# The looped last pair of experts in the order of the straight chunks

## The chip, the cores and the metric

The kernel runs on one core of a Trainium2 chip. The metric is device time in microseconds (us), from the first to the last instruction of one execution. Three executions of the kernel before took 1598.59, 1598.82 and 1604.25 us; their median is 1598.82 us.

## The reference, cut to what matters

The router picks 2 of 16 experts for each token. Two decoder layers with the same shape run one after the other over 576 tokens (512 of a prompt, 64 of a sample group). Each layer is a block of token mixers followed by a mixture of experts, with a layer norm after either. The change touches only the mixture of experts:

```python
def moe_ffn(h, w_router, b_router, w_gate, w_up, w_down):
    ...
    hg = jnp.einsum('ntd,edf->ntef', h, w_gate)
    hu = jnp.einsum('ntd,edf->ntef', h, w_up)
    act = jax.nn.silu(hg) * hu * combine[..., None].astype(h.dtype)
    return jnp.einsum('ntef,efd->ntd', act, w_down)
x = layer_norm(DN_ALPHA * x + f, lw['ln2_g'], lw['ln2_b'])   # f = moe_ffn(x, ...)
```

The width is 1024, an expert's hidden width 256, and all of it is float32.

## The kernel before

Tokens are sorted by expert into chunks of up to 128 rows, each chunk with one expert. Chunks 0 to 15 always exist, one per expert; an expert with more rows gets more chunks behind these. How many there are is only known when the router has run, so the first 14 chunks (`STATIC`) are written out straight, and the rest run in a hardware loop over pairs of chunks, whose trip count each engine reads from the tile `plan` (`pairs`, L1639). With these inputs the trip count is 1 in each layer: the page counts 32 gate-and-up loads in two layers. So a layer has chunks 0 to 15, and chunks 14 and 15 are the loop's only pair.

What a chunk n needs, and which engine does it (functions of `experts`, L1572):

- SP loads the gate and up weights (`load_gu`, 2 MB) and the down weights (`load_dw`, 1 MB), each into one of three slots.
- POOL gathers the chunk's rows from HBM by an indirect DMA (`gather`) and at the end adds the result rows into the output in HBM by another one (`scatter`). Scatters must not overlap, since two may add to one row: each waits until the one before has landed (`y_stored`).
- PE transposes the rows (`rows_t`, called for the chunk behind by `next_rows_t`), does the gate-and-up product (`gate_up`, 24 matmuls), transposes the hidden rows (`hidden_t`) and does the down product (`down`, 8 matmuls) into one pair of PSUM banks.
- ACT makes the high parts of the weights (`gate_up_high`, 4 casts: each float32 operand is split into a high and a low part) and of the rows (`rows_high`), the tanh of the gate (`gate_tanh`), the copy of the transposed hidden rows (`hidden_copy`) and the copy of the result out of PSUM (`output_copy`, which waits for the landing of the scatter two chunks back, since it overwrites its source).
- DVE makes the low parts of the weights and rows (`gate_up_low`, `rows_low`) and finishes the hidden rows (`hidden`).

The program writes every engine's order out by hand; semaphores do the rest. In the straight chunks the order is staggered. PE does `gate_up(n)`, `hidden_t(n-1)`, `next_rows_t(n)`, `down(n-1)`, and ACT and DVE split the weights of chunk n+1 while PE works on chunk n. In the loop it is not: chunk 13 is finished ahead of the loop, then the weights of 14 and 15 are split one after the other, and each of the two chunks goes through `gate_up`, `next_rows_t`, `hidden_t`, `down` before the next starts.

On POOL, which the change leaves as it is, the straight chunks gather four chunks ahead while there are straight chunks to gather for, and the loop, for a = 0 and 1, gathers chunk 16 + a and then scatters chunk 14 + a (L1856 to 1873):

```python
for n in range(STATIC):
    if n + 4 < STATIC + 2:
        pool.wait_ge(xt_done, n + 3)
        gather(n % 2, table[:, 0, n + 4:n + 5])
    pool.wait_ge(y_out, n + 1)
    ...
    scatter(n % 2, table[:, 1, n:n + 1])
with pool.Fori(0, pairs(pool)) as p:
    for a in range(2):
        ...
```

So straight chunks 12 and 13 gather nothing, and the gather for chunk 16 stands behind the scatter of chunk 13. Chunk 16 has no rows here, but PE transposes its (stale) row buffer all the same: `next_rows_t` of chunk 15 waits on `rows_in_a` for that gather.

When the last scatter has landed, SP reloads the summed rows (L2076), and the layer norm behind them begins.

Of the kernel before, what the change touches and what calls it, by code (L numbers as in the profile page):

```python
# [14 lines left out]
F32 = mybir.dt.float32  # L15
# [44 lines left out]
MAXCH = 24  # L60
# [5 lines left out]
for _n, _w in [("ident", 128), ("diag", 128), ("cos", NTT * 8), ("sin", NTT * 8), ("cm", NT * 32), ("cneg", NT * 32),  # L66
               ("newneg", 2 * 64), ("scneg", 2 * 128), ("bcur0", 4 * 128), ("bcur", 4 * 128), ("bprev", 4 * 128),
               ("bst", 4 * 64), ("bnew", 4 * 64), ("tri", 128), ("ones", 128), ("pairm", 32), ("th", 5),
               ("chunk", 32), ("gm", 128), ("gms", 64), ("blk", 4), ("rowhead", 4), ("mhalf", NTT), ("gsel", 256), ("lane", 128), ("row1", 1), ("tile128", 2 * NTT),
               ("pad", 2 * (MAXCH + 2)), ("e128", 16), ("over", 16), ("fix", 32)]:  # L70
    _C[_n] = (_at, _at + _w)
    _at += _w
# [12 lines left out]
def constants():  # L85
# [60 lines left out]
    put("tile128", np.tile(128 * (np.arange(2 * NTT) % NTT), (128, 1)))  # L146
    put("over", np.tile(128 * (15 - np.arange(16)), (128, 1)))
# [1408 lines left out]
class Chunk:  # L1556


    def __init__(self, n, slot, side, half, nth):
        self.n, self.slot, self.side, self.half, self.nth = n, slot, side, half, nth  # L1560


def fixed_chunk(c):
    return Chunk(c, c % RING_E, c % 2, c // 2, c // RING_E + 1)


def looped_chunk(p, a):
    c = STATIC + a
    return Chunk(p * 2 + c, c % RING_E, a, p + c // 2, p + (c // RING_E + 1))


def experts(k):  # L1572
# [18 lines left out]
    with ExitStack() as outer:  # L1591
# [4 lines left out]
        plan = so("plan", [1, 34], I32)  # L1596
        with ExitStack() as ctx:
# [14 lines left out]
            big, pf = sb("cmpbuf", [1, 32, E]), sb("plan_f", [1, 34])  # L1612
# [32 lines left out]
            def _(sp):  # L1645
                def load_gu(ch, e):
                    sp.dma_start(gu[:, ch.slot, :], io["we"][l, e, :, 0:4096]).then_inc(gu_in[ch.slot], 16)

                def load_dw(ch, e):
                    sp.dma_start(dw[:, ch.slot, :], io["we"][l, e, :, 4096:6144]).then_inc(dw_in[ch.slot], 16)  # L1650
                load_dw(fixed_chunk(2), 2)
                norm.load(sp)
                for n in range(RING_E, STATIC + 1):
                    if n < STATIC:
                        sp.wait_ge(gu_done, n - RING_E + 1)
                        load_gu(fixed_chunk(n), n)
# [15 lines left out]
            def _(pe):  # L1672
# [58 lines left out]
                def down(ch, first=False):  # L1731
# [4 lines left out]
                    pe.wait_ge(dw_in[ch.slot], ch.nth * 16)  # L1736
                    for n in range(2):
                        for f in range(2):
                            last = pe.matmul(ps[:, YB + n, :], hT[:, f, :],  # L1739
                                             dw[:, ch.slot, f * D + n * 512:f * D + (n + 1) * 512],  # L1740
# [12 lines left out]
                hidden_t(fixed_chunk(STATIC - 1))  # L1753
                down(fixed_chunk(STATIC - 1))
                with pe.Fori(0, pairs(pe)) as p:
                    for a in range(2):
                        ch = looped_chunk(p, a)
                        gate_up(ch)
                        next_rows_t(ch)
                        hidden_t(ch)  # L1760
                        down(ch)

            @block.scalar
            def _(act):
# [5 lines left out]
                def gate_up_high(ch, early=False, begin=0):  # L1770
                    act.wait_ge(gu_in[ch.slot], ch.nth * 16)
# [3 lines left out]
                    for q in range(begin, PIECES):  # L1775
                        cols = slice(q * PW, (q + 1) * PW)
                        act.copy(guH[ch.side][:, cols], gu[:, ch.slot, cols]).then_inc(w_hi, 1)  # L1777
# [98 lines left out]
            def _(dve):  # L1876
# [41 lines left out]
                def gate_up_low(ch, pieces=(0, 1, 2, 3)):  # L1918
                    for q in pieces:
                        cols = slice(q * PW, (q + 1) * PW)  # L1920
                        dve.wait_ge(w_hi, ch.n * PIECES + (q + 1))
                        dve.tensor_tensor(guL[:, ch.slot, cols], gu[:, ch.slot, cols], guH[ch.side][:, cols].bitcast(F32),  # L1922
# [58 lines left out]
                def plan_chunks():  # L1981
# [12 lines left out]
                    step(dve.memset(pf[:, 33:34], 0.0))  # L1994
# [194 lines left out]
```

## Time and profile before

| | us |
|---|---|
| median of three executions | 1598.82 |
| the profiled execution's own time | 1600.21 |
| span of its trace | 1598.5 |
| PE busy in the span (matmul) | 1411.0 |
| DVE busy | 780.1 |
| ACT busy | 607.6 |
| POOL busy | 178.1 |

The span is the stretch from the first to the last instruction in the trace. The experts of layer 1 lie between 565 and 775 us, those of layer 2 between 1363 and 1569 us. Below, "scatter 12" is the twelfth counted from 0, that of chunk 12, and so for all steps; POOL issues the scatters of even chunks from `y_a` and those of odd ones from `y_b`. A row of a timeline gives the start, the duration, the engine, the line, the operation with its tiles, how many were merged, and in brackets how long the engine had been idle and what ended that. For a DMA the duration is that of its issue; when its data have landed stands in the answers on DMA, in us from the issue.

### The profile page before, as it was taken

The numbers are of one execution on the slowest core, as the hardware profiler recorded it, in microseconds if no ns is written. First come the engines' busy times: TensorE is split into PE (matmuls) and PEld (weight loads), VectorE is DVE, ScalarE is ACT, GpSimd is POOL, SyncE is SP. The second block draws the span as 40 slices with busy tenths as digits, with TensorE's granted clock in tenths as the row PEclk, the third lists the DMA queues.
The fourth block names the chain that finished last, engine by engine and source line by source line (L and its number), as shares of the span: only waits on it lengthen the run. The fifth ranks groups of instructions, "written<-read, shape, count | busy, mean of one in ns | idle before, by whom it ended". The sixth has DMA issues, their size and how long they took to land. (4 is left out here: it accounts for less than half of the span.)

```text
span 1598.5 us, 22710 instructions
## 1 busy us (share of the span) xinstructions
PE 1411.0 (88%) x9068; PEld 1156.1 (72%) x9068; DVE 780.1 (49%) x1294; ACT 607.6 (38%) x1142; POOL 178.1 (11%) x154
## 2 busy tenths in 40 slices
PE   7999897999999779987289998979999997799960
PEld 6897565999997657664178975659999976576640
DVE  3225666433334776553532256664333357765535
ACT  3332677222221246553223326772222212465530
POOL 3021000000000112222130210000000001122221
PEclk9999998999999879998589999989999998899995
DMA  8234301222225759975352142012222257599843
GB/s 272 73 120 157 103 2 70 76 84 89 85 61 196 278 174 354 340 246 143 115 177 64 57 160 100 2 70 81 79 90 86 61 203 270 176 353 323 291 116 126
DMA packets 55860, 236.69 MB, mean 148 GB/s; under 512 B 11690, under 2 KB 19768, under 8 KB 46220
## 3 DMA queue, kind: packets, MB, share of 16 engines
q1 hardware_dynamic: 44428, 211.88, 37.4%
q0 software_dynamic: 11328, 23.38, 6.3%
q8 instruction: 72, 1.18, 0.3%
q14 instruction: 32, 0.26, 0.1%
HBM read 219.30 MB, written 36.58 MB: 160 GB/s over the span
## 5 line engine op out<-in xcount | busy, mean ns | idle before, releaser
L1355 PE MATMUL ps<-xT_high,w_high 128*128 128x288 f32 x768 | 229.8, 299 | 16.3 <-DVE w_ring_low L1481 16.3
L1356 PE MATMUL ps<-xT_low,w_high 128*128 128x288 f32 x768 | 228.1, 297 | 0.0
L1357 PE MATMUL ps<-xT_high,w_ring_low 128*128 128x288 f32 x768 | 227.2, 296 | 0.0
L1355 PEld LDWEIGHTS ps<-xT_high,w_high 128*128 128x128 f32 x768 | 146.3, 190 | 18.4 <-DVE w_ring_low L1481 18.0
L1454 ACT ACTIVATE tanh_gate<-ps 128x576 f32<-128x576 f32 x48 | 31.3, 653 | 304.0 <-PE ps L1357 304.0
L1356 PEld LDWEIGHTS ps<-xT_low,w_high 128*128 128x128 f32 x768 | 146.7, 191 | 0.0
L1357 PEld LDWEIGHTS ps<-xT_high,w_ring_low 128*128 128x128 f32 x768 | 146.7, 191 | 0.0
L499 PE MATMUL ps<-z_w_high_part,oT_low 128*128 128x454 f32 (+1 forms) x320 | 120.3, 376 | 14.1 <-DVE z_w_ring_low L967 14.1
L1739 PE MATMUL ps<-down,hidT 128*128 128x512 f32 x256 | 118.4, 606 | 6.1 <-ACT hidT L1790 2.6
L501 PE MATMUL ps<-z_w_high_part,xT_low 128*128 128x454 f32 (+1 forms) x320 | 119.4, 373 | 0.0
L500 PE MATMUL ps<-z_w_ring_low,oT_low 128*128 128x454 f32 (+1 forms) x320 | 119.2, 372 | 0.0
L1236 POOL TENSOR_TENSOR ln_rs<-ln_mv,const 128x1 f32<-128x1 f32 (+1 forms) x20 | 19.7, 983 | 868.7 <-DVE ln_mv L1231 868.7
L1509 DVE SCALAR_TENSOR_TENSOR branch_part<-tanh_gate,ps 128x576 f32<-128x576 f32 x32 | 24.1, 754 | 180.0 <-ACT tanh_gate L1454 180.0
L967 DVE TENSOR_TENSOR z_w_ring_low<-z_w_ring,z_w_high_part 128x908 fp32r<-128x908 f32 (+1 forms) x40 | 44.1, 1102 | 136.0 <-ACT z_w_high_part L810 136.0
L1722 PE MATMUL ps<-gate_up_low,rowsT_high 128*128 128x512 f32 x256 | 103.3, 403 | 0.0
L1922 DVE TENSOR_TENSOR gate_up_low<-gate_up,oT_low 128x1024 fp32r<-128x1024 f32 x58 | 67.3, 1220 | 61.4 <-ACT oT_low L1777 61.4
L1481 DVE TENSOR_TENSOR w_ring_low<-w_ring,w_high 128x1280 fp32r<-128x1280 f32 (+2 forms) x56 | 85.7, 1530 | 17.1 <-ACT w_high L1436 15.6
L1922 DVE TENSOR_TENSOR gate_up_low<-gate_up,xT_low 128x1024 fp32r<-128x1024 f32 x64 | 74.1, 1218 | 35.3 <-ACT xT_low L1777 35.1
L1739 PEld LDWEIGHTS ps<-down,hidT 128*128 128x128 f32 x256 | 47.3, 195 | 55.2 <-issue 52.3
L1105 DVE TENSOR_REDUCE row_max<-ps 128x2 f32<-128x1024 f32 (+3 forms) x76 | 60.8, 802 | 54.0 <-PE ps L662 42.6
L901 ACT ACTIVATE probs<-ps,row_max 128x128 f32<-128x128 f32 (+4 forms) x152 | 77.9, 521 | 15.3 <-DVE row_max L1105 14.8
L1436 ACT CAST w_high<-w_ring 128x1280 fp32r<-128x1280 f32 (+2 forms) x56 | 72.2, 1290 | 14.2 <-PE ps L1357 9.6
(324 smaller groups left out, 3052.2 us busy)
## 6 DMA issues: line engine op xcount, KB each, us to landing
gate_up<-in_we SPq DMA_DIRECT2D x32, 2048.0 KB, 11.5
down<-in_we SPq DMA_DIRECT2D x32, 1024.0 KB, 10.3
w_ring<-in_wm SPq DMA_DIRECT2D x32, 640.0 KB, 4.2
z_w_ring<-in_wtm SPq DMA_DIRECT2D x32, 454.0 KB, 3.9
w_ring<-in_wm SPq DMA_DIRECT2D x16, 768.0 KB, 4.5
w<-in_w SPq DMA_DIRECT2D x2, 2048.0 KB, 8.7
sel_pages<-in_sel_pages SPq DMA_DIRECT2D x32, 128.0 KB, 2.0
win_rows<-in_win_rows SPq DMA_DIRECT2D x2, 2048.0 KB, 7.9
```

Of the source, the lines that this page charges most:

```text
L499: pe.matmul(out, w[0], x[0], start=first, stop=False)
L500: pe.matmul(out, w[0], x[1], start=False, stop=False)
L501: return pe.matmul(out, w[1], x[0], start=False, stop=last)
L901: act.activation(P[:, m % 3, h, 0:w], ps[:, bank + h, 0:w], ACT.Exp, bias=mx[:, m % 3, h:h + 1], accum_out=den[:, m % 3, h:h + 1]).then_in ...
L1355: pe.matmul(out, w[0], x[0], start=first, stop=False)
L1356: pe.matmul(out, w[0], x[1], start=False, stop=False)
L1357: return pe.matmul(out, w[1], x[0], start=False, stop=last)
L1436: act.copy(wh[:, u % HRING, 0:width[u]], w32[:, u % RING, 0:width[u]]).then_inc(w_hi, 1)
L1481: return dve.tensor_tensor(low, src, high.bitcast(F32), ALU.subtract)
L1722: last = pe.matmul(out, xTH[:, kk, :], guL[:, ch.slot, cols], start=False, stop=(kk == KT_D - 1))
L1739: last = pe.matmul(ps[:, YB + n, :], hT[:, f, :], dw[:, ch.slot, f * D + n * 512:f * D + (n + 1) * 512], start=(f == 0), stop=(f == 1))
L1922: dve.tensor_tensor(guL[:, ch.slot, cols], gu[:, ch.slot, cols], guH[ch.side][:, cols].bitcast(F32), ALU.subtract).then_inc(w_lo, 1)
```

## The change

On PE, ACT and DVE the loop takes the straight chunks' order: the down product one chunk behind the gate-and-up product, the splits one chunk ahead. Chunk 13 is no longer finished ahead of the loop but in its first half; chunk 15 is finished behind the loop. For the loads this means that SP's straight part now also loads the gate and up weights of chunk 14, that the loop loads 15 and then 16 (a chunk that is not there with one pair; its weights are loaded and split, and used by nothing), and that slots are numbered anew. A small table (`pairgate`) gives the load of chunk 15 its wait. POOL's instructions are the same as before.

```diff
 def looped_chunk(p, a):
-    c = STATIC + a
-    return Chunk(p * 2 + c, c % RING_E, a, p + c // 2, p + (c // RING_E + 1))
+    n, half = p * 2 + (STATIC + a), p + (STATIC + a) // 2
+    if a % 2:
+        return Chunk(n, 1, half, 0, p + (a // 2 + 6), 0, 1, p + (a // 2 + 6))
+    return Chunk(n, 0, half, 1, p + (a // 2 + 5), 2, 2, p + (a // 2 + 5))
...
                 for n in range(RING_E, STATIC + 1):
-                    if n < STATIC:
-                        sp.wait_ge(gu_done, n - RING_E + 1)
-                        load_gu(fixed_chunk(n), n)
+                    sp.wait_ge(gu_done, n - RING_E + 1)
+                    load_gu(fixed_chunk(n), n)
                     if n > RING_E:
                         sp.wait_ge(dn_done, n - RING_E)
                         load_dw(fixed_chunk(n - 1), n - 1)
                 with sp.Fori(0, pairs(sp)) as p:
-                    two = [looped_chunk(p, a) for a in range(2)]
-                    e = [sp.value_load(plan[0:1, bass.ds(ch.n, 1)], min_val=0, max_val=E - 1) for ch in two]
-                    for a in range(2):
-                        sp.wait_ge(gu_done, two[a].n - 1)
-                        load_gu(two[a], e[a])
-                    for a in range(2):
-                        sp.wait_ge(dn_done, two[a].n - 1)
-                        load_dw(two[a], e[a])
+                    even, odd, after = looped_chunk(p, 0), looped_chunk(p, 1), looped_chunk(p, 2)
+                    e = [sp.value_load(plan[0:1, bass.ds(ch.n, 1)], min_val=0, max_val=E - 1) for ch in (even, odd, after)]
+                    gate = sp.value_load(plan[0:1, bass.ds(p + 34, 1)], min_val=STATIC - 1, max_val=STATIC + 10)
+                    sp.wait_ge(gu_done, gate)
+                    load_gu(odd, e[1])
+                    sp.wait_ge(dn_done, even.n - 1)
+                    load_dw(even, e[0])
+                    sp.wait_ge(gu_done, gate + 1)
+                    load_gu(after, e[2])
+                    sp.wait_ge(dn_done, odd.n - 1)
+                    load_dw(odd, e[1])
...
-                hidden_t(fixed_chunk(STATIC - 1))
-                down(fixed_chunk(STATIC - 1))
-                with pe.Fori(0, pairs(pe)) as p:
+                count = pairs(pe)
+                with pe.Fori(0, count) as p:
                     for a in range(2):
-                        ch = looped_chunk(p, a)
-                        gate_up(ch)
-                        next_rows_t(ch)
-                        hidden_t(ch)
-                        down(ch)
+                        gate_up(looped_chunk(p, a))
+                        hidden_t(looped_chunk(p, a - 1))
+                        next_rows_t(looped_chunk(p, a))
+                        down(looped_chunk(p, a - 1))
+                hidden_t(looped_chunk(count, -1))
+                down(looped_chunk(count, -1))
...
                 for n in range(STATIC):
-                    if n + 1 < STATIC:
-                        gate_up_high(fixed_chunk(n + 1), n + 1 < 2)
+                    gate_up_high(fixed_chunk(n + 1), n + 1 < 2)
                     if n:
                         hidden_copy(fixed_chunk(n - 1))
                     rows_high(n + 2)
                     gate_tanh(fixed_chunk(n))
                     if n:
                         output_copy(fixed_chunk(n - 1), n - 1 < 2)
-                hidden_copy(fixed_chunk(STATIC - 1))
-                output_copy(fixed_chunk(STATIC - 1))
-                with act.Fori(0, pairs(act)) as p:
-                    two = [looped_chunk(p, a) for a in range(2)]
-                    gate_up_high(two[0])
+                count = pairs(act)
+                with act.Fori(0, count) as p:
                     for a in range(2):
-                        if a == 0:
-                            gate_up_high(two[1])
-                        gate_tanh(two[a])
-                        rows_high(two[a].n + 2)
-                        hidden_copy(two[a])
-                        output_copy(two[a])
+                        ch, ago = looped_chunk(p, a), looped_chunk(p, a - 1)
+                        gate_up_high(looped_chunk(p, a + 1))
+                        hidden_copy(ago)
+                        rows_high(ch.n + 2)
+                        gate_tanh(ch)
+                        output_copy(ago)
+                hidden_copy(looped_chunk(count, -1))
+                output_copy(looped_chunk(count, -1))
...
                 for n in range(STATIC):
-                    if n + 1 < STATIC:
-                        gate_up_low(fixed_chunk(n + 1))
+                    gate_up_low(fixed_chunk(n + 1))
                     rows_low(n + 2)
                     hidden(fixed_chunk(n), wslot[:, n:n + 1])
                     if n == 1:
                         plan_chunks()
                 with dve.Fori(0, pairs(dve)) as p:
-                    two = [looped_chunk(p, a) for a in range(2)]
-                    gate_up_low(two[0])
                     for a in range(2):
-                        if a == 0:
-                            gate_up_low(two[1])
+                        ch = looped_chunk(p, a)
+                        if a:
+                            dve.wait_ge(gu_done, ch.n)
+                        gate_up_low(looped_chunk(p, a + 1))
+                        rows_low(ch.n + 2)
                         dve.tensor_copy(wcol[:, a:a + 1], wslot[:, bass.ds(p * 2 + (STATIC + a), 1)]).then_inc(wcol_ready, 1)
                         dve.wait_ge(wcol_ready, p * 2 + (a + 1))
-                        hidden(two[a], wcol[:, a:a + 1])
-                        rows_low(two[a].n + 2)
+                        hidden(ch, wcol[:, a:a + 1])
```

How the instructions move is shown at two places. The first is PE, from the end of the gate-and-up product of chunk 15 to the end of its part of the experts. L1704 before and L1715 after are the row transposes for chunk 16, L1728 and L1739 the transposes of the hidden rows (`hid_a` is chunk 14, `hid_b` chunk 15), L1739 and L1750 the down products. Before:

```order
L1722 MATMUL ps<-gate_up_low,rowsT_high 128x512
L1709 ISA
L1704 MATMUL ps<-const,rows_a 128x128 [waits rows_in_a]
L1704 MATMUL ps<-const,rows_a 128x128 x7
L1726 REGISTER_ALU
L1728 MATMUL ps<-const,hid_b 128x128 [waits hidden_ready]
L1728 MATMUL ps<-const,hid_b 128x128
L1736 ISA [waits hiddenT_out,y_out]
L1739 MATMUL ps<-down,hidT 128x512 [waits down_in0]
L1739 MATMUL ps<-down,hidT 128x512 x3
```

And the same place in the kernel after:

```order
L1739 MATMUL ps<-const,hid_a 128x128 [waits hidden_ready]
L1739 MATMUL ps<-const,hid_a 128x128
L1720 ISA
L1715 MATMUL ps<-const,rows_a 128x128 [waits rows_in_a]
L1715 MATMUL ps<-const,rows_a 128x128 x7
L1750 MATMUL ps<-down,hidT 128x512 [waits down_in2,hiddenT_out,y_out]
L1750 MATMUL ps<-down,hidT 128x512 x3
...
L1739 MATMUL ps<-const,hid_b 128x128 [waits hidden_ready]
...
L1747 ISA [waits hiddenT_out,y_out]
L1750 MATMUL ps<-down,hidT 128x512 [waits down_in1]
L1750 MATMUL ps<-down,hidT 128x512 x3
```

The down product of chunk 14 stood ahead of these rows before; now it stands behind the transposes that wait for the gather of chunk 16.

The second place is SP's queue, from the last straight chunk's loads on. Before:

```order
L1647 DMA gate_up<-in_we 128x4096 [waits gate_up_done]
L1650 DMA down<-in_we 128x2048 [waits down_done] x2
L1642 TENSOR_LOAD plan [waits plan_ready]
...
L1647 ISA [waits gate_up_done]
L1647 DMA gate_up<-in_we 128x4096
...
L1650 ISA [waits down_done]
L1650 DMA down<-in_we 128x2048
```

Of the loop's rows the first load of each kind is shown, and there are two of each, both gate-and-up loads first. After:

```order
L1653 DMA gate_up<-in_we 128x4096 [waits gate_up_done]
L1656 DMA down<-in_we 128x2048 [waits down_done]
L1648 TENSOR_LOAD plan [waits plan_ready]
...
L1653 ISA [waits gate_up_done]
L1653 DMA gate_up<-in_we 128x4096
...
L1656 ISA [waits down_done]
L1656 DMA down<-in_we 128x2048
```

One more gate-and-up load stands ahead of the loop, that of chunk 14, and in the loop the two kinds take turns: 15, down 14, gate and up of 16, down 15.

## Rows read from the trace of the kernel before

**Rows 1.** DMA issues, page: name, count, KB each, median us to landing

```profile
gate_up<-in_we SPq DMA_DIRECT2D x32, 2048.0 KB, 11.5
```

**Rows 2.** Timeline of SP, layer 1: start us, us, what was issued, count

```profile
710.08 10.40 SPq L1647 DMA_DIRECT2D gate_up<-in_we  x2
724.66 5.49 SPq L1650 DMA_DIRECT2D down<-in_we  x2
775.27 2.48 SPq L2076 DMA_DIRECT2D x<-expert_rows  x5
```

**Rows 3.** Timeline of POOL, layer 1: start, us, what, [idle before <-releaser]

```profile
703.75 1.59 POOL L1838 DMA_INDIRECT expert_rows<-y_b,slot_table  x1 [4.15 <-DMA expert_rows<-y_a,slot_table]
...
712.93 1.59 POOL L1838 DMA_INDIRECT expert_rows<-y_a,slot_table  x1 [6.24 <-DMA expert_rows<-y_b,slot_table]
...
722.54 1.59 POOL L1838 DMA_INDIRECT expert_rows<-y_b,slot_table  x1 [6.67 <-DMA expert_rows<-y_a,slot_table]
734.50 1.57 POOL L1838 DMA_INDIRECT expert_rows<-y_a,slot_table  x1 [10.38 <-DMA expert_rows<-y_b,slot_table]
741.39 1.65 POOL L1838 DMA_INDIRECT expert_rows<-y_b,slot_table  x1 [5.32 <-DMA expert_rows<-y_a,slot_table]
...
744.82 1.16 POOL L1834 DMA_INDIRECT rows_a<-x_rows,row_idx_a  x1 [0.91 <-POOL row_idx_a L1843]
...
754.48 1.60 POOL L1838 DMA_INDIRECT expert_rows<-y_a,out_idx_a  x1 [0.83 <-POOL out_idx_a L1843]
...
766.29 1.59 POOL L1838 DMA_INDIRECT expert_rows<-y_b,out_idx_b  x1 [0.83 <-POOL out_idx_b L1843]
```

**Rows 4.** Landings of the transfers issued at 741 to 766 us

```profile
expert_rows<-y_b,slot_table POOLq DMA_INDIRECT x1, 6.3
rows_a<-x_rows,row_idx_a POOLq DMA_INDIRECT x1, 3.1
expert_rows<-y_a,out_idx_a POOLq DMA_INDIRECT x1, 6.5
```

**Rows 5.** Landings of all 32 scatters, by source line

```profile
DMA to landing us min/median/max: 6.0/10.2/13.6
```

**Rows 6.** Landings of the transfers issued at 1467 to 1490 us

```profile
expert_rows<-y_b,slot_table POOLq DMA_INDIRECT x1, 10.4
```

**Rows 7.** Timeline of PE, layer 1, last pair and the stage behind

```profile
737.13 0.80 PE L1720 MATMUL ps<-oT_low,rowsT_high 128*128 128x512 f32 x1 [7.47 <-DVE gate_up_low L1922]
...
748.32 3.69 PE L1739 MATMUL ps<-down,hidT 128*128 128x512 f32 x8 [0.65 <-ACT hidT L1790]
...
783.18 1.97 PE L1264 MATMUL ps<-const,x 128*128 128x128 f32 x8 [19.29 <-DVE x L1253]
```

**Rows 8.** Timeline of ACT, layer 1, last pair

```profile
733.73 0.59 ACT L1797 COPY y_b<-ps 128x512 f32<-128x512 f32 x1 [7.84 <-DMA expert_rows<-y_b,slot_table]
...
738.57 3.88 ACT L1777 CAST xT_low<-gate_up 128x1024 fp32r<-128x1024 f32 x4
```

**Rows 9.** Busy times by stretch: us and counts by engine, PEclk, DMA, GB/s

```profile
702.00:712.00 10.00, 10.00 (x43) 7.07 (x42) 7.08 (x10) 6.20 (x10) 2.63 (x2) 1.00 0.62 180
737.00:741.00 4.00, 3.87 (x9) 3.10 (x10) 4.00 (x5) 4.00 (x5) 0.00 (x0) 0.50 0.37 60
```

**Rows 10.** Timeline of DVE, layer 1, last pair

```profile
740.40 4.62 DVE L1922 TENSOR_TENSOR gate_up_low<-gate_up,xT_low 128x1024 fp32r<-128x1024 f32 x4
```

**Rows 11.** Timeline of POOL, layer 2

```profile
1529.57 1.57 POOL L1838 DMA_INDIRECT expert_rows<-y_a,slot_table  x1 [10.42 <-DMA expert_rows<-y_b,slot_table]
1538.21 3.24 POOL L1838 DMA_INDIRECT expert_rows<-y_b,slot_table  x1 [7.08 <-issue]
...
1560.18 1.59 POOL L1838 DMA_INDIRECT expert_rows<-y_b,out_idx_b  x1 [0.84 <-POOL out_idx_b L1843]
```

**Rows 12.** Landings of the scatters issued at 1529 to 1539 us

```profile
expert_rows<-y_a,slot_table POOLq DMA_INDIRECT x1, 7.5
expert_rows<-y_b,slot_table POOLq DMA_INDIRECT x1, 7.8
```

More of the change, by code:

```diff
@@ L69 @@
                ("chunk", 32), ("gm", 128), ("gms", 64), ("blk", 4), ("rowhead", 4), ("mhalf", NTT), ("gsel", 256), ("lane", 128), ("row1", 1), ("tile128", 2 * NTT),
-               ("pad", 2 * (MAXCH + 2)), ("e128", 16), ("over", 16), ("fix", 32)]:
+               ("pad", 2 * (MAXCH + 2)), ("e128", 16), ("over", 16), ("fix", 32), ("pairgate", 6)]:
     _C[_n] = (_at, _at + _w)
@@ L146, in constants @@
     put("tile128", np.tile(128 * (np.arange(2 * NTT) % NTT), (128, 1)))
+    put("pairgate", np.tile(np.where(np.arange(6) == 0, STATIC - 1, STATIC + 2 * np.arange(6)), (128, 1)))
     put("over", np.tile(128 * (15 - np.arange(16)), (128, 1)))
@@ L1556, with __init__ @@
 class Chunk:
-    def __init__(self, n, slot, side, half, nth):
-        self.n, self.slot, self.side, self.half, self.nth = n, slot, side, half, nth
+    def __init__(self, n, side, half, raw, raw_nth, slot, dslot, d_nth):
+        self.n, self.side, self.half = n, side, half
+        self.raw, self.raw_nth, self.slot = raw, raw_nth, slot
+        self.dslot, self.d_nth = dslot, d_nth
 def fixed_chunk(c):
-    return Chunk(c, c % RING_E, c % 2, c // 2, c // RING_E + 1)
+    return Chunk(c, c % 2, c // 2, c % RING_E, c // RING_E + 1, c % RING_E, c % RING_E, c // RING_E + 1)
 def looped_chunk(p, a):
-    c = STATIC + a
-    return Chunk(p * 2 + c, c % RING_E, a, p + c // 2, p + (c // RING_E + 1))
+    n, half = p * 2 + (STATIC + a), p + (STATIC + a) // 2
+    if a % 2:
+        return Chunk(n, 1, half, 0, p + (a // 2 + 6), 0, 1, p + (a // 2 + 6))
+    return Chunk(n, 0, half, 1, p + (a // 2 + 5), 2, 2, p + (a // 2 + 5))
 def experts(k):
@@ L1595, in experts @@
         norm = Norm(k, "ln2", 2, EPS / ALPHA ** 2, outer)
-        plan = so("plan", [1, 34], I32)
+        plan = so("plan", [1, 40], I32)
         with ExitStack() as ctx:
@@ L1611, in experts @@
             cum, cumx = sb("cum", [1, 1]), sb("cum_before", [128, E + 1])
-            big, pf = sb("cmpbuf", [1, 32, E]), sb("plan_f", [1, 34])
+            big, pf = sb("cmpbuf", [1, 32, E]), sb("plan_f", [1, 40])
             with ExitStack() as routing:
@@ L1646, in load_gu @@
                 def load_gu(ch, e):
-                    sp.dma_start(gu[:, ch.slot, :], io["we"][l, e, :, 0:4096]).then_inc(gu_in[ch.slot], 16)
+                    sp.dma_start(gu[:, ch.raw, :], io["we"][l, e, :, 0:4096]).then_inc(gu_in[ch.raw], 16)
                 def load_dw(ch, e):
-                    sp.dma_start(dw[:, ch.slot, :], io["we"][l, e, :, 4096:6144]).then_inc(dw_in[ch.slot], 16)
+                    sp.dma_start(dw[:, ch.dslot, :], io["we"][l, e, :, 4096:6144]).then_inc(dw_in[ch.dslot], 16)
                 load_dw(fixed_chunk(2), 2)
@@ L1735, in down @@
                     pe.wait_ge(ht_out, ch.n + 1)
-                    pe.wait_ge(dw_in[ch.slot], ch.nth * 16)
+                    pe.wait_ge(dw_in[ch.dslot], ch.d_nth * 16)
                     for n in range(2):
@@ L1739, in down @@
                             last = pe.matmul(ps[:, YB + n, :], hT[:, f, :],
-                                             dw[:, ch.slot, f * D + n * 512:f * D + (n + 1) * 512],
+                                             dw[:, ch.dslot, f * D + n * 512:f * D + (n + 1) * 512],
                                              start=(f == 0), stop=(f == 1))
@@ L1770, in gate_up_high @@
                 def gate_up_high(ch, early=False, begin=0):
-                    act.wait_ge(gu_in[ch.slot], ch.nth * 16)
+                    act.wait_ge(gu_in[ch.raw], ch.raw_nth * 16)
                     if not early:
@@ L1776, in gate_up_high @@
                         cols = slice(q * PW, (q + 1) * PW)
-                        act.copy(guH[ch.side][:, cols], gu[:, ch.slot, cols]).then_inc(w_hi, 1)
+                        act.copy(guH[ch.side][:, cols], gu[:, ch.raw, cols]).then_inc(w_hi, 1)
                 def rows_high(count):
@@ L1921, in gate_up_low @@
                         dve.wait_ge(w_hi, ch.n * PIECES + (q + 1))
-                        dve.tensor_tensor(guL[:, ch.slot, cols], gu[:, ch.slot, cols], guH[ch.side][:, cols].bitcast(F32),
+                        dve.tensor_tensor(guL[:, ch.slot, cols], gu[:, ch.raw, cols], guH[ch.side][:, cols].bitcast(F32),
                                           ALU.subtract).then_inc(w_lo, 1)
@@ L1993, in plan_chunks @@
                     step(dve.tensor_scalar(pf[:, 32:33], pf[:, 32:33], 1.0, None, ALU.add))
-                    step(dve.memset(pf[:, 33:34], 0.0))
+                    dve.memset(pf[:, 33:34], 0.0)
+                    step(dve.tensor_copy(pf[:, 34:40], c["pairgate"][0:1, :]))
                     dve.tensor_copy(plan[:, :], pf[:, :]).then_inc(plan_ready, 1)
```

## The prediction

> **What bounds the kernel now.** I read the page's busy shares first: PE is busy 88% of the span, so a change to the order on PE is worth what it takes from PE's idle stretches or from the path that ends a stage. Then I read the timelines of POOL, PE, ACT and SP in the last pair of layer 1, and POOL's again in layer 2. The stage ends when scatter 15 has landed and SP reloads the rows, at 775.27 us [rows 2], 9.0 after that scatter was issued [rows 3]. So the question for each layer is: when is scatter 15 issued? Nothing behind it changes.
>
> The reader is to see a chain in POOL's timeline [rows 3]. Scatters 9, 10, 11, 12 and 13 start at 703.75, 712.93, 722.54, 734.50 and 741.39, and each waits for the landing of the one before it (the releasers in brackets). A scatter starts about 0.8 after the landing before it: scatter 11 landed near 733.7, which is also when ACT's copy of chunk 13 was let go after 7.84 idle [rows 8]. How long a landing takes depends on what else the DMA engines carry: of all 32, the shortest took 6.0 and the longest 13.6 [rows 5], one in the middle of the straight chunks of layer 2 took 10.4 [rows 6], and with the weights all loaded it is 6.3 and 6.5 [rows 4].
>
> Because ACT waited for scatter 11, it split the weights of chunk 14 late, and PE stood idle 7.47 us before that chunk's gate-and-up product [rows 7]. From there PE and ACT go one step at a time, and scatters 14 and 15 wait for the computation, at 754.48 and 766.29 [rows 3]. This idle PE time is what the new order can fill.
>
> **What the change removes.** By the new order chunk 14's weights are split while chunk 13's products run, so the 7.47 of idle PE goes, and chunk 15's product need not wait for chunk 14's result. What is late next is the chain of scatters, and one wait that was hidden before.
>
> **The moved wait.** PE's transposes for chunk 16 wait for its gather, and now stand ahead of the down product of 14. On POOL, unchanged, this gather stands behind scatter 13: it was issued at 744.82, 3.4 after that scatter [rows 3], and landed 3.1 later [rows 4], at 747.9, just behind the scatter (741.39 + 6.3 = 747.7). Before, PE came to these transposes only behind down 14, which started at 748.32 [rows 7], and did not notice. Now it comes to them earlier. Down 12 is through by 724.66, when SP issues the load that waits for it [rows 2]; a whole chunk keeps PE busy for some 10 us (10.00 of 10 from 702 to 712 [rows 9]), so chunk 13's down product ends near 734.5, and gate-and-up 15 about 6 us of the next 10 later, near 741 by estimate. There PE stops, and everything behind the transposes waits with it: down 14, scatter 14, and behind the pair down 15. The rows that it waits for are used by nothing.
>
> **The moved loads.** The two gate-and-up loads of the pair went out at 710.08 and about 720.1 [rows 2]. Now chunk 14's goes out a chunk earlier, near 700, chunk 15's at 710.1, and a third, for chunk 16, behind the down weights of 14 near 725: 2 MB per layer that were not there. The stretch from 702 to 712 had the DMA engines busy only 0.62 of the time [rows 9]; it was the gap in which scatters 9 and 10 were quick (8.3 and 8.8: the next starts less 0.8 [rows 3]). That gap is filled.
>
> **The chain worked out, layer 1.** Scatter 8 landed at 702.9 (703.75 less 0.85); with a load beside its last 3 us, 704.0 (between 702.9 and 706). Scatter 9 starts at 704.8 and, beside weights all the way, takes 10.4 [rows 6]: 715.2. Scatter 10 starts at 716.0; chunk 15's load ends about 721.6 (710.1 + 11.5 [rows 1]), so 5.6 of 10.4 pass beside it and the other 46% at the free rate of 6.0 [rows 5]: 724.4. Scatter 11 starts at 725.2, beside the down load of 14 and the load of 16; it took 11.1 before beside the like: 736.3, which is 2.6 later than before. Scatter 12 at 737.1 has the last down load beside it. Before it took 6.1 in layer 1 (734.50 to 741.39 less 0.8) and 7.5 in layer 2 [rows 12]; in between I take 7.5, since the last down load now goes out about 5 us later: 744.6. Scatter 13 at 745.4 takes 6.3: 751.7, and the gather of 16 lands at 751.9.
>
> Then the tail. PE has been idle some 11 us. Behind 7.47 us of idle it ran at half speed (PEclk 0.50, its 1.2 GHz level) for 4 us at least [rows 7, 9], and eight transposes behind 19.29 of idle took 1.97 [rows 7]; so 2.0 for the transposes, and for the down product 3.7 [rows 7] plus 1.1 for some 2.2 us left at half speed, 4.8. From the end of down 14 (748.32 + 3.69 = 752.0) to scatter 14 at 754.48 it was 2.5 [rows 3, 7]; its landing takes 6.5 [rows 4], and the lookup ahead of scatter 15 is 1.3 by estimate, 0.83 of it in the row [rows 3]. Chunk 15's hidden rows, down product and copies fit into the landing with about 2 to spare. Sum: 2.0 + 4.8 + 2.5 + 6.5 + 1.3 = 17.1, so scatter 15 starts at 751.9 + 17.1 = 769.0, against 766.29: 2.7 later.
>
> **Layer 2.** Scatter 11 landed at 1528.7 (1529.57 less 0.85 [rows 11]). The same 2.6 later is 1531.3; scatter 12 at 1532.1 lands at 1539.6, scatter 13 at 1540.4 lands at 1546.7, the gather at 1546.9, and scatter 15 starts at 1564.0 against 1560.18 [rows 11]: 3.8 later.
>
> **Added work that is hidden.** Per layer four casts on ACT, 3.88 together [rows 8], and four subtractions on DVE, 4.62 together [rows 10], split chunk 16's weights; they fall between chunk 13's copy and the wait above, where ACT and DVE have some 11 us free. Without that cover they would cost 4.6. The few register loads and the plan's extra copy are below 1 us and stand ahead of engines that wait.
>
> **The sum.** 2.7 + 3.8 = 6.5 us. The profiled execution took 1600.21 (its span is 1598.5), and would take 1606.7; it stands 1.4 above the median of 1598.82, so the forecast against the median is 1605.3.
>
> The trace shows a scatter of 10.4 beside weight loads and one of 6.3 without [rows 4, 6]. The Trainium skill, in "DMA: Bandwidth & Descriptors", section "Rules for kernel authors", advises to issue a DMA early, compute meanwhile, and wait for it late. By that rule the earlier loads would cost nothing and the scatters would keep their old times, which gives the second rival's 1600.6; by the rows the sum stands at 1605.3.
>
> **Rivals.** First, faster: PE doesn't stop at the transposes, because the gather of 16 is there in time. Then scatters alone set the pace: 14 at 751.7 + 1.3 = 753.0, 15 at 753.0 + 6.5 + 1.3 = 760.8, 5.5 earlier than before; in layer 2, 1546.7 + 9.1 = 1555.8, 4.4 earlier: 1588.9. With scatters as quick as before it would be 747.7 + 9.1 and 1546.0 + 9.1, 14.6 in all, 1584.2. For it speaks the idle PE [rows 7]; against it POOL's order, which puts that gather behind scatter 13.
>
> Second, the loads in the gap cost the scatters nothing: 9 to 13 land as before, the gather at 747.9 and, in layer 2, at 1546.2 (1538.21 + 7.8 [rows 11, 12] + 0.2). With the tail of 17.1, scatter 15 starts at 765.0 and 1563.3: 1.3 earlier and 3.1 later, 1600.6. For it speaks the DMA share of 0.62 [rows 9]; against it the spread of the landings [rows 5].
>
> Third, slower by more: the scatters of the last chunks sink to the worst landing. Scatters 9 and 11 at 13.6 [rows 5] put 9 at 718.4, 10 at 726.5 (2.4 us of it loaded) and 11 at 740.9, 4.6 later than in the forecast; both layers together 15.7, 1614.5. It decides from the point where scatter 9 takes more than the 10.4 assumed. For it speaks the third gate-and-up load; against it that layer 2 held 10.4 in its straight chunks [rows 6].
>
> **How the numbers follow.** The forecast gets 0.52, its own range 1599 to 1611; the faster rival 0.12, the free loads 0.18, the worst landings 0.18. A measurement of this kernel tells 0.5%, 8.0 us, from no change: below 1590.8 is faster, above 1606.8 slower. Faster: 0.10 of the first rival. Slower: 0.18, and 0.19 of the forecast's upper part: 0.37. Within: the rest, 0.53. The range 1590 to 1613 leaves out about half of the first rival and part of the third.
>
> **What would show it.** In the profile after: PE idle for 8 to 13 us ahead of chunk 16's transposes (now L1715), with the gather of `rows_a` as releaser; chunk 14's gate-and-up product right behind the down product of 12, without the idle of 7.47; scatters 9 and 10 above 10 and 8; scatter 15 of layer 1 near 769. The forecast is wrong if PE doesn't wait there, or if scatter 13 starts as early as 741.

## The result, and the profile after

The kernel after took 1605.82 us (median of 20 runs, 1599.08 to 1611.04); the kernel before, run beside it, 1599.7 (20 runs, 1594.25 to 1604.25 and a single one at 4855.73, which a median does not feel). The ratio is 1.0035, with a 95% interval of 1.0022 to 1.0048: about 0.35% slower. The forecast was 1605.3, in a range from 1590 to 1613.

The profiled execution of the kernel after took 1601.55 us, 4.3 below that median, while the one of before took 1600.21, 0.5 above its own. So the two traces differ by only 1.3, and what they show of single stages is read with that in mind; how much a cause is worth is taken from the ratios of the experiments.

The page of the kernel after: busy times, and the loads of gate and up weights.

```profile
span 1599.9 us, 22752 instructions
...
PE 1407.9 (88%) x9068; PEld 1155.1 (72%) x9068; DVE 789.6 (49%) x1304; ACT 614.2 (38%) x1150; POOL 177.3 (11%) x154
...
gate_up<-in_we SPq DMA_DIRECT2D x34, 2048.0 KB, 11.5
```

There are 34 such loads now, where it was 32 [rows 1]: one more per layer, for a chunk that is not there. DVE is 9.5 us busier and ACT 6.6; the splits of those weights take 4.63 per layer on DVE and 3.89 on ACT, which is about that much.

The timeline of PE around the last pair, layer 1 and then layer 2 (start, duration, engine, line, what, and in brackets the idle time before and what ended it), answers to [rows 7].

```profile
719.75 3.60 PE L1750 MATMUL ps<-down,hidT 128*128 128x512 f32 x8
722.79 0.80 PE L1731 MATMUL ps<-oT_low,rowsT_high 128*128 128x512 f32 x1
...
747.14 1.97 PE L1715 MATMUL ps<-const,rows_a 128*128 128x128 f32 x8 [7.82 <-DMA rows_a<-x_rows,row_idx_a]
748.90 4.09 PE L1750 MATMUL ps<-down,hidT 128*128 128x512 f32 x8
...
754.68 3.70 PE L1750 MATMUL ps<-down,hidT 128*128 128x512 f32 x8 [1.48 <-ACT hidT L1801]
...
1545.64 1.97 PE L1715 MATMUL ps<-const,rows_a 128*128 128x128 f32 x8 [11.26 <-DMA rows_a<-x_rows,row_idx_a]
1547.40 4.20 PE L1750 MATMUL ps<-down,hidT 128*128 128x512 f32 x8
```

The idle 7.47 ahead of chunk 14's gate-and-up product [rows 7] is gone: down 12 starts at 719.75 and gate-and-up 14 follows at 722.79, with no idle time in brackets. In its place PE stands 7.82 us in layer 1 and 11.26 in layer 2 ahead of the transposes for chunk 16, and what lets it go is the gather of `rows_a`. Only then comes the down product of chunk 14.

POOL's timeline in layer 1 answers to [rows 3], the landings below it to [rows 4, 5] (us from the issue, of scatters 9 to 13 and of the gather).

```profile
702.11 1.59 POOL L1847 DMA_INDIRECT expert_rows<-y_b,slot_table  x1 [4.59 <-DMA expert_rows<-y_a,slot_table]
...
714.72 1.59 POOL L1847 DMA_INDIRECT expert_rows<-y_a,slot_table  x1 [9.68 <-DMA expert_rows<-y_b,slot_table]
...
722.12 1.59 POOL L1847 DMA_INDIRECT expert_rows<-y_b,slot_table  x1 [3.96 <-DMA expert_rows<-y_a,slot_table]
731.23 1.57 POOL L1847 DMA_INDIRECT expert_rows<-y_a,slot_table  x1 [7.53 <-DMA expert_rows<-y_b,slot_table]
740.39 1.80 POOL L1847 DMA_INDIRECT expert_rows<-y_b,slot_table  x1 [7.60 <-DMA expert_rows<-y_a,slot_table]
...
743.30 1.09 POOL L1843 DMA_INDIRECT rows_a<-x_rows,row_idx_a  x1 [0.91 <-POOL row_idx_a L1852]
754.43 0.18 POOL L1852 COPY out_idx_a<-slot_table 128x1 int32 x1 [10.04 <-ACT y_a L1809]
755.45 1.60 POOL L1847 DMA_INDIRECT expert_rows<-y_a,out_idx_a  x1 [0.84 <-POOL out_idx_a L1852]
...
763.16 1.59 POOL L1847 DMA_INDIRECT expert_rows<-y_b,out_idx_b  x1 [0.83 <-POOL out_idx_b L1852]
```

```profile
expert_rows<-y_b,slot_table POOLq DMA_INDIRECT x1, 11.8
...
expert_rows<-y_a,slot_table POOLq DMA_INDIRECT x1, 6.5
...
expert_rows<-y_b,slot_table POOLq DMA_INDIRECT x1, 8.3
...
expert_rows<-y_a,slot_table POOLq DMA_INDIRECT x1, 8.4
...
expert_rows<-y_b,slot_table POOLq DMA_INDIRECT x1, 6.5
...
rows_a<-x_rows,row_idx_a POOLq DMA_INDIRECT x1, 3.8
```

The scatters still follow one another from landing to landing, and the gather of 16 lands at 743.30 + 3.8 = 747.1, when PE goes on. Scatter 14 then waits 10.04 for ACT's copy of its result: a wait for the computation, which itself waited for POOL. In layer 2 (answering to [rows 11]) the same chain is longer; the first row is scatter 9.

```profile
1498.45 1.59 POOL L1847 DMA_INDIRECT expert_rows<-y_b,slot_table  x1 [8.96 <-DMA expert_rows<-y_a,slot_table]
...
1517.31 1.59 POOL L1847 DMA_INDIRECT expert_rows<-y_b,slot_table  x1 [3.62 <-DMA expert_rows<-y_a,slot_table]
1527.23 1.57 POOL L1847 DMA_INDIRECT expert_rows<-y_a,slot_table  x1 [8.33 <-DMA expert_rows<-y_b,slot_table]
1539.20 1.55 POOL L1847 DMA_INDIRECT expert_rows<-y_b,slot_table  x1 [10.40 <-issue]
...
1561.42 1.59 POOL L1847 DMA_INDIRECT expert_rows<-y_b,out_idx_b  x1 [0.84 <-POOL out_idx_b L1852]
```

Scatters 11 and 12 take 9.9 and 12.0 here from issue to the next issue, against 9.1 and 9.2 in layer 1. What they run beside is in SP's timeline of layer 1 (answering to [rows 2]): after chunk 15's load the down weights of 14, the gate and up weights of 16, and the down weights of 15.

```profile
708.00 0.35 SPq L1653 DMA_DIRECT2D gate_up<-in_we  x1
723.53 0.34 SPq L1656 DMA_DIRECT2D down<-in_we  x1
724.13 0.33 SPq L1653 DMA_DIRECT2D gate_up<-in_we  x1
733.68 0.33 SPq L1656 DMA_DIRECT2D down<-in_we  x1
```

A useful length is that from the issue of scatter 8 to the issue of scatter 15, the stretch that the change touches. By the traces it was 70.1 (layer 1) and 71.2 (layer 2) before, 141.3 together, and is 69.1 and 75.4 after, 144.4: 3.1 longer, all of it in layer 2. Below, "the stretch" is this sum of both layers.

### The profile page after: what moved, and what is told of

Read it like the earlier page. It is cut to its first block and busy times, and to the rows that moved or that the text cites. A ratio compares the mean times of both kernels' runs of the same rounds, so it can differ in the third digit from the quotient of the medians.

```text
span 1599.9 us, 22752 instructions
## 1 busy us (share of the span) xinstructions
PE 1407.9 (88%) x9068; PEld 1155.1 (72%) x9068; DVE 789.6 (49%) x1304; ACT 614.2 (38%) x1150; POOL 177.3 (11%) x154
## 5 line engine op out<-in xcount | busy, mean ns | idle before, releaser
L1356 PEld LDWEIGHTS ps<-xT_high,w_high 128*128 128x128 f32 x768 | 145.9, 190 | 18.5 <-DVE w_ring_low L1482 18.1
L1750 PE MATMUL ps<-down,hidT 128*128 128x512 f32 x256 | 118.8, 608 | 3.9 <-ACT hidT L1801 3.0
L1931 DVE TENSOR_TENSOR gate_up_low<-gate_up,oT_low 128x1024 fp32r<-128x1024 f32 x66 | 76.5, 1220 | 52.6 <-ACT oT_low L1788 52.6
L1482 DVE TENSOR_TENSOR w_ring_low<-w_ring,w_high 128x1280 fp32r<-128x1280 f32 (+2 forms) x56 | 85.7, 1530 | 17.1 <-ACT w_high L1437 15.6
L1750 PEld LDWEIGHTS ps<-down,hidT 128*128 128x128 f32 x256 | 47.8, 197 | 52.6 <-issue 52.5
```

The source lines that it names most:

```text
L1356: pe.matmul(out, w[0], x[0], start=first, stop=False)
L1482: return dve.tensor_tensor(low, src, high.bitcast(F32), ALU.subtract)
L1750: last = pe.matmul(ps[:, YB + n, :], hT[:, f, :], dw[:, ch.dslot, f * D + n * 512:f * D + (n + 1) * 512], start=(f == 0), stop=(f == 1))
L1931: dve.tensor_tensor(guL[:, ch.slot, cols], gu[:, ch.raw, cols], guH[ch.side][:, cols].bitcast(F32), ALU.subtract).then_inc(w_lo, 1)
```

## The experiments

Two theories stood against each other. G: the order does save time, and the wait for the gather of chunk 16 takes it back. L: the loads do it, those of 14 and 15 that go out a chunk earlier and the third one, because they lengthen the scatters. Each is compared with the kernel before, run beside it on the same chip: e1 to e4 on one chip, beside a median of 1598.01, e5 to e8 on another, beside 1595.91. All ratios have 95% intervals.

**e1, the gather a chunk earlier.** On POOL the straight part gathers for one chunk more, so that the gather of 16 stands ahead of scatter 12, and the loop gathers for 17 and 18 in place of 16 and 17. The tables get one entry more, and the last wait on `x_in` is adapted.

```diff
-                    if n + 4 < STATIC + 2:
+                    if n + 4 < STATIC + 3:
...
-                        pool.wait_ge(xt_done, ch.n + 1)
-                        gather(a, looked_up(idx[a], 0, p * 2 + (STATIC + a + 2)))
+                        pool.wait_ge(xt_done, ch.n + 2)
+                        gather(1 - a, looked_up(idx[1 - a], 0, p * 2 + (STATIC + a + 3)))
```

> The kernel after, with POOL gathering one chunk further ahead: chunk 16's rows are asked for ahead of scatter 12 instead of behind scatter 13, those of chunk 17 ahead of scatter 14 (the lookup tables get one more column for it). Theory G (PE waits for the gather of chunk 16, and that wait eats what the new order gains): the idle of 7.82 and 11.26 us ahead of chunk 16's transposes goes; scatter 14 follows scatter 13's landing by 1.3 us and scatter 15 that of 14, about 7 us earlier per layer than in the kernel after: ratio to the kernel before 0.994 to 0.996 (about 1592 us). Theory L (the earlier and the added loads are what costs, through longer scatters): PE no longer waits there, but the last scatters come no earlier: ratio 1.002 to 1.004, as the kernel after.

Measured: 1586.46 us, ratio 0.993 (0.9915 to 0.9944). That is faster than both kernels; against the kernel after it is 0.993 / 1.0035 = 0.9895, some 17 us. PE and then POOL of e1 in layer 1:

```profile
737.34 1.04 PE L1715 MATMUL ps<-const,rows_a 128*128 128x128 f32 x8
738.78 3.67 PE L1750 MATMUL ps<-down,hidT 128*128 128x512 f32 x8 [0.41 <-issue]
```

```profile
722.63 1.04 POOL L1843 DMA_INDIRECT rows_a<-x_rows,slot_table  x1 [0.31 <-issue]
734.32 1.59 POOL L1847 DMA_INDIRECT expert_rows<-y_a,slot_table  x1 [10.64 <-DMA expert_rows<-y_b,slot_table]
741.33 1.57 POOL L1847 DMA_INDIRECT expert_rows<-y_b,slot_table  x1 [5.42 <-DMA expert_rows<-y_a,slot_table]
...
747.38 0.18 POOL L1852 COPY out_idx_a<-slot_table 128x1 int32 x1 [2.29 <-DMA expert_rows<-y_b,slot_table]
748.39 1.60 POOL L1847 DMA_INDIRECT expert_rows<-y_a,out_idx_a  x1 [0.84 <-POOL out_idx_a L1852]
...
755.58 1.59 POOL L1847 DMA_INDIRECT expert_rows<-y_b,out_idx_b  x1 [0.83 <-POOL out_idx_b L1852]
```

Scatter 13 starts at 741.33, no earlier than the 740.39 of the kernel after. But PE no longer stops for the gather, its transposes take 1.04 in place of 1.97, down 14 is done at 742.5, and what releases scatter 14 is now the landing of 13. Scatters 14 and 15 follow at 7.1 and 7.2 us. G holds, and it was worth more than expected. The windows from the transposes on, of the kernel after and of e1, show the clock (third from last): 0.64 granted behind 7.82 us of idle, part of it at the lower level of 1.2 GHz, and 1.00 where PE had not stopped.

```profile
747.00:751.00 4.00, 3.86 (x12) 2.73 (x13) 1.24 (x3) 1.36 (x3) 0.00 (x0) 0.64 0.02 4
```

```profile
737.00:743.00 6.00, 5.48 (x22) 2.68 (x20) 5.40 (x8) 3.37 (x7) 1.67 (x2) 1.00 0.23 45
```

**e4, the control.** The same edit on POOL, put into the kernel before.

> The kernel before, with the same edit on POOL as the first of these runs: chunk 16's rows gathered ahead of scatter 12. Theory G: in the old order PE comes to chunk 16's transposes when the gather has long landed, so the edit is worth nothing there: ratio 0.999 to 1.001. If POOL's order were worth something by itself (fewer steps between the last two scatters), the ratio would fall below 0.999 here too, and the first run would say nothing on PE's wait.

Measured: 1597.31, ratio 0.9997 (0.9985 to 1.0009). The earlier gather is worth nothing where PE comes to those transposes behind down 14. So the gain of e1 is that of the wait which the new order had exposed.

**e2, without the third load.** In the kernel after the load of chunk 16 is cut from 4096 columns to 64, and its splits with it.

```diff
-                    load_gu(after, e[2])
+                    sp.dma_start(gu[:, after.raw, 0:64], io["we"][l, e[2], :, 0:64]).then_inc(gu_in[after.raw], 16)
...
-                        gate_up_high(looped_chunk(p, a + 1))
+                        gate_up_high(looped_chunk(p, a + 1), PW=16 if a else PW)
...
-                        gate_up_low(looped_chunk(p, a + 1))
+                        gate_up_low(looped_chunk(p, a + 1), PW=16 if a else PW)
```

> The kernel after, with the load of chunk 16's gate and up weights cut from 4096 to 64 columns and its splits to 64 columns; with one pair per layer nothing uses chunk 16, so only unused work is left out (with more pairs it would not be right). Theory G: scatters 11 and 12 run beside 2 MB less and land 1 to 2 us earlier per layer, the wait for the gather stays: ratio to before 1.000 to 1.003. Theory L with the third load as the cause: the whole loss goes and the ratio falls below 0.999.

Measured: 1593.49, ratio 0.9975 (0.9962 to 0.9987); against the kernel after 0.994, some 9.5 us. G's expectation was missed: the third load costs something too. POOL of e2 in layer 1, and then the windows of 12 us from the place of that load, first of e2 and then of the kernel after (the last three columns are the granted clock, the DMA engines' busy share and GB/s):

```profile
723.16 1.59 POOL L1847 DMA_INDIRECT expert_rows<-y_b,slot_table  x1 [3.26 <-DMA expert_rows<-y_a,slot_table]
730.08 1.59 POOL L1847 DMA_INDIRECT expert_rows<-y_a,slot_table  x1 [5.33 <-DMA expert_rows<-y_b,slot_table]
736.87 1.55 POOL L1847 DMA_INDIRECT expert_rows<-y_b,slot_table  x1 [5.20 <-DMA expert_rows<-y_a,slot_table]
```

```profile
725.00:737.00 12.00, 12.00 (x52) 8.58 (x51) 7.38 (x13) 7.78 (x16) 1.72 (x2) 1.00 0.67 158
```

```profile
724.00:736.00 12.00, 12.00 (x52) 8.58 (x51) 6.89 (x9) 7.10 (x11) 1.57 (x1) 1.00 0.96 300
```

Without the load the DMA engines are 0.67 busy instead of 0.96, and from scatter 11 to scatter 13 it is 736.87 - 723.16 = 13.7 us, where the kernel after takes 740.39 - 722.12 = 18.3. In layer 2 it is 15.7 against 21.9. Together that is 10.8, near the 9.5 of the ratios. The Trainium skill, in "DMA: Bandwidth & Descriptors", section "Queues, rings and completion order", says that each DMA engine takes turns between the queues that have work for it, a packet at a time. The traces fit this: scatters 11 and 12 took 8.3 and 8.4 beside that load in layer 1 and 6.1 and 6.0 without it, in layer 2 9.1 and 10.9 against 7.9 and 5.8. The turns themselves are shown by no view here.

How does a longer scatter reach PE? By the wait, as the idle time by releaser ahead of L1715 shows, both layers together: the kernel after, then e2.

```profile
  DMA rows_a<-x_rows,row_idx_a: 19.1, 2
```

```profile
  DMA rows_a<-x_rows,row_idx_a: 6.7, 2
```

In e1 no such line is left. So the two costs are no independent terms: the load delays scatters 11 to 13, behind which the gather stands, and the wait passes the delay on.

**e8, the load without the splits.** As e2, but with the load of chunk 16 whole and only its splits cut.

> The kernel after with the full load of chunk 16 but its splits on ACT and DVE cut to 64 columns (right for one pair per layer). If the 2 MB load is what cost in the run without both: ratio as the kernel after, 1.002 to 1.005. If the splits on ACT and DVE cost (8.5 us of work per layer, beside the wait): 0.996 to 0.999.

Measured: 1603.14, ratio 1.0043 (1.0028 to 1.0057), as slow as the kernel after. So it is the 2 MB and not the work on ACT and DVE.

**e3, the loads held back.** The kernel after with the loads of 14, 15 and 16 issued one chunk later, the first two at about the times of before (708.91 and 719.13, against 710.08 and some 720.1 [rows 2]).

```diff
-    put("pairgate", np.tile(np.where(np.arange(6) == 0, STATIC - 1, STATIC + 2 * np.arange(6)), (128, 1)))
+    put("pairgate", np.tile(np.where(np.arange(6) == 0, STATIC, STATIC + 2 * np.arange(6)), (128, 1)))
...
-                    sp.wait_ge(gu_done, n - RING_E + 1)
+                    sp.wait_ge(gu_done, n - RING_E + 1 + (n == STATIC))
```

> The kernel after, with the gate and up loads of chunks 14, 15 and 16 held back by one chunk each, so that 14 and 15 go out when they did in the kernel before. Theory G: scatter 9 is quick again (8 to 9 us instead of 11 to 12), scatter 11 starts up to 2 us earlier but has more loads beside it; the wait for the gather stays: ratio to before 1.000 to 1.004. Theory L with the earlier loads as the cause: the loss goes, ratio below 0.999.

Measured: 1604.22, ratio 1.0042 (1.0024 to 1.0059). Holding them back gains nothing. Scatter 9 of layer 1 was quick, as expected (5.7), but scatters 10 and 11 took 11.8 and 11.1: the long landings moved to where the loads went. The third load moved as well (from 724.13 to 731.27), so this run alone does not set 14 and 15 apart from it; the next one does.

**e5, the reverse.** The kernel before with the loads of 14 and 15 one chunk earlier, and nothing else. In its text M takes these earlier loads for a cost, N for none.

```diff
-                    if n < STATIC:
-                        sp.wait_ge(gu_done, n - RING_E + 1)
-                        load_gu(fixed_chunk(n), n)
+                    sp.wait_ge(gu_done, n - RING_E + 1)
+                    load_gu(fixed_chunk(n), n)
...
-                    for a in range(2):
-
-                        sp.wait_ge(gu_done, two[a].n - 1)
-                        load_gu(two[a], e[a])
+                    sp.wait_ge(gu_done, two[1].n - 2)
+                    load_gu(two[1], e[1])
```

> The kernel before, in its own order, with the gate and up loads of chunks 14 and 15 sent one chunk earlier, as in the kernel after, and no load for chunk 16 (right for one pair per layer). Theory M (loads that fill the gap at 700 to 710 us lengthen scatters 9 and 10, and by the chain all behind them): ACT's wait for scatter 11 ends 1 to 3 us later per layer: ratio 1.001 to 1.004. Theory N (the gap was free; only the third load costs): ratio 0.999 to 1.001.

Measured: 1598.09, ratio 1.0011 (0.9997 to 1.0026). This doesn't tell M from N; it says that the earlier loads cost 0.26% at most, 4 us. In the traces, the start of scatter 12 less that of scatter 8 is 40.2 in layer 1 and 40.8 in layer 2, against 38.3 and 40.6 before: later by something in M's range in one layer, by 0.2 in the other. POOL of e5 in layer 1 (scatters 9 to 12) shows why it is no more.

```profile
702.42 1.59 POOL L1835 DMA_INDIRECT expert_rows<-y_b,slot_table  x1 [7.96 <-DMA expert_rows<-y_a,slot_table]
...
715.50 1.59 POOL L1835 DMA_INDIRECT expert_rows<-y_a,slot_table  x1 [9.65 <-DMA expert_rows<-y_b,slot_table]
...
722.19 1.59 POOL L1835 DMA_INDIRECT expert_rows<-y_b,slot_table  x1 [3.75 <-DMA expert_rows<-y_a,slot_table]
731.25 1.57 POOL L1835 DMA_INDIRECT expert_rows<-y_a,slot_table  x1 [7.47 <-DMA expert_rows<-y_b,slot_table]
```

From scatter 9 to scatter 11 it is 19.8 (19.4 in layer 2), where it was 18.8 (17.2) before; but from 11 to 12 it is 9.1 (9.6), where it was 12.0 in both layers. What scatters 9 and 10 lose, scatter 11 gives back.

**e6, both costs taken away.** The edits of e1 and e2 together, in the kernel after.

> The kernel after with both edits: chunk 16's rows gathered ahead of scatter 12, and chunk 16's load and splits cut to 64 columns (right for one pair per layer). If the two costs lie one behind the other on the chain of scatters, they add: 0.993 less 0.006 gives 0.986 to 0.988 (about 1578 us). If the computation of chunk 15 becomes the end of the path once the scatters are quicker, less is left of the second: 0.989 to 0.992.

Measured: 1580.54, ratio 0.9893 (0.9872 to 0.9914). Its interval spans both expectations. With the wait gone, the load is worth 0.9893 / 0.993, some 0.4%, where it was 0.6% with the wait; the intervals don't separate these two. What ends last in its layer 1 is the computation again:

```profile
748.65 0.18 POOL L1852 COPY out_idx_a<-slot_table 128x1 int32 x1 [5.77 <-ACT y_a L1809]
749.66 1.60 POOL L1847 DMA_INDIRECT expert_rows<-y_a,out_idx_a  x1 [0.83 <-POOL out_idx_a L1852]
```

Scatter 14 waits for ACT's copy of its rows, behind a down product that PE reached at 743.60 without a stop.

**e7, no loop at all.** The kernel before with `STATIC = 16` and the loop over pairs left out: chunks 14 and 15 in the straight order, no chunk 16 touched by PE, and no load for it. It fits these inputs only.

```diff
-STATIC = 14
+STATIC = 16
...
-                with pe.Fori(0, pairs(pe)) as p:
+                for p in ():
```

> The kernel before with 16 straight chunks and no loop (right where an expert has at most 128 rows in these inputs; a further chunk would be left out). The straight code gathers chunk 16 ahead of scatter 12 and has no load for it, so it is the order of the change without its two costs: as the run with both edits, within 0.002 of it, 0.985 to 0.990. If the loop itself (register waits, lookups) cost more than 2 us per layer, it would be below 0.985.

Measured: 1579.49, ratio 0.9884 (0.9864 to 0.9904). This is what the order is worth here with neither cost and without the loop: 1.2%, or 18.5 us, near the 17 of e6. The stretch was 141.3 before, 144.4 after, and by the traces 126.6 in e1, 135.9 in e2, 120.4 in e6 and 124.5 in e7. Each is one execution (that of e7 stands 6.2 above its median, that of e2 5.1 below), so these sums show where the time lies and the ratios how much it is.

## Why the prediction came out right

**The sum.** Forecast 6.5 us slower; measured 1605.82 - 1599.7 = 6.1. The time and the main mechanism hold, but of the terms behind them one was too large and one too small, and in the profiled execution the loss lies in one layer, not in both.

**The moved wait: right.** PE stands ahead of chunk 16's transposes, released by the gather, for 7.8 (just short of the range) and 11.3 us against 8 to 13 forecast, and the 7.47 is gone. e1 shows that this wait decides: without it the change is a gain of 0.7%. The rival in which PE doesn't stop was put at 1588.9; e1, which makes it true, took 1586.46.

**The moved loads: the step that failed is the 11.1 of scatter 11 ("it took 11.1 before beside the like").** That the gap fills up held: scatter 9 took longer (11.8 and, in layer 2, 11.0), 10 was quick (6.5 and 6.2), and from the start of 9 to that of 11 it was 20.0 and 18.9, against 18.8 and 17.2 before and 20.4 in the sum. But the load that stood beside scatter 11 had left. In layer 1 chunk 15's load went out at 720.1 before and took 11.0; now it goes out at 708.00 and has landed after 10.5, ahead of scatter 11 at 722.12. So scatter 11 took 8.3 and 9.1 in place of 11.1 and 11.2. The start of scatter 12 less that of scatter 8 went from 38.3 to 37.2 in layer 1 and from 40.6 to 41.2 in layer 2: no 2.6. e5, which moves these loads alone, shows the same exchange and no cost that can be told from none. The load that costs is the third: scatter 12 took 8.4 and 10.9 where 7.5 stood in the sum, and 6.0 and 5.9 in e5. e2 and e8 show what it costs in all, some 9.5 us. The forecast counted that load only as the reason for 11.1 at scatter 11. So 2.8 and 2.0 too much at scatter 11 stood against 0.9 and 3.4 too little at scatter 12, and that these two came near to cancelling was luck.

**The tail: near.** From the landing of the gather to scatter 15 it is 763.16 - 747.1 = 16.1 in layer 1 and, from PE's release, 1561.42 - 1545.64 = 15.8 in layer 2, against 17.1. The down product behind the half-speed transposes took 4.09 and 4.20, not 4.8; the rest is PE's two steps overlapping by 0.2. The 2.0 for the transposes, 2.5 to scatter 14 and 7.8 from there to scatter 15 are 1.97, 2.46 and 7.71.

**Scatter 15 of layer 1 "near 769": missed** in the profiled execution, where it is at 763.16; layer 2 has 1561.42 for 1564.0. Scatter 8 of layer 1 was itself 2.1 earlier than in the trace of before, ahead of the first load that the change moves; that of layer 2 was 3.0 earlier, about the 3.1 by which layer 1 had ended earlier; and that execution is 4.3 faster than its median. Single landings vary by more than the terms of the sum (scatter 11 of e1 took 12.7 in layer 1 and 7.7 in layer 2); a forecast to 3 us at one place of one trace could not be met by more than luck.

**The hidden splits: right.** ACT's casts for chunk 16 end at 740.07, just after PE's wait begins (747.14 - 7.82 = 739.3), and before its next casts, those of the rows, ACT is idle for 8.80; e8, without these splits, is no faster:

```profile
736.18 3.89 ACT L1788 CAST oT_low<-gate_up 128x1024 fp32r<-128x1024 f32 x4 [1.56 <-DMA gate_up<-in_we]
...
749.14 1.07 ACT L1793 CAST rowsT_high<-ps 128x512 fp32r<-128x512 f32 x2 [8.80 <-PE ps L1715]
```

**The rivals.** Free loads (1600.6): half true; moving the two loads is about free, the third is not. The advice of the Trainium skill, in "DMA: Bandwidth & Descriptors", "Rules for kernel authors", to issue a DMA early agrees with e5, where the earlier loads cost 0.26% at most. The third load, which nothing uses, cost 0.6% (e2). Worst landings (1614.5): not seen. Scatter 9 did take more than the 10.4 from which that rival was to decide, but 10 and 11 came out quicker than it has them; the longest scatter of the trace took 13.1, before 13.6 [rows 5].

**What stays open.** Where the 0.6% of the third load and the wait overlap is known only roughly, from e6. A gather behind scatter 12, one chunk later than in e1, was not tried. A kernel that keeps the loop for any number of pairs and yet leaves out the load of chunk 16 was not tried.

## What to carry to other kernels

When work is put in a pipelined order, list every wait that it moves ahead of something urgent, and ask on which queue the awaited transfer stands and behind what: here a gather that nobody needed, behind a scatter on an unchanged queue, turned a gain of 0.7% (e1) into a loss of 0.35%. The repair is to gather one chunk further ahead on POOL, with tables one entry longer, and belongs to the same change. A prefetch of something that may not exist isn't free where a serial chain of small transfers sets the end: price it by how much that chain's landings grow beside it, not by whether its consumers have time.

## What the runs showed of the hardware

- In no trace did a gather land ahead of the scatter that POOL had issued just before it. In the kernel after, behind scatter 13, it landed just behind: 743.30 + 3.8 = 747.1 against 740.39 + 6.5 = 746.9. In e1, behind scatter 11, it was 734.2 against 733.4 in layer 1, but 1522.4 against 1518.1 in layer 2. So the landing of the scatter was the earliest time for the gather, and at times it came later.
- Beside the third load, of 2 MB, scatters 11 and 12 together took 16.0 to 20.0 us (both layers of the kernel after, e1 and e8); without it, with the loads of 14 and 15 at the same early place, 12.0 to 14.6 (e2, e5 and e6). The loads of chunks 14 and 15 themselves, issued a chunk earlier (e5) or with the third one later (e3), moved the total by no more than could be measured.
